# Eight router logits per token written with tokens on the partitions, two VectorE steps moved, and products that nobody reads in three waits of TensorE

## What is computed

```python
def moe_swiglu(h, router, w_in, w_out):
    logits = jnp.einsum('bnd,de->bne', h, router).astype(jnp.float32)
    top_logit, top_idx = lax.top_k(logits, TOP_K)          # TOP_K = 2 of N_EXPERTS = 8
    top_w = jax.nn.softmax(top_logit, axis=-1)
    gates = jnp.sum(jax.nn.one_hot(top_idx, N_EXPERTS, dtype=jnp.float32) * top_w[..., None], axis=-2)
    out = jnp.zeros_like(h)
    for e in range(N_EXPERTS):
        out = out + gates[..., e:e + 1].astype(h.dtype) * swiglu(h, w_in[e], w_out[e])
    return out
```

## Time and profile before

| | us |
|---|---|
| median of three runs | 1781.78 |
| lowest, highest | 1780.74, 1786.87 |
| the profiled execution, whole | 1783.62 |
| its span in the profile | 1781.9 |
| TensorE busy in it | 1682.8 (94%) |
| part from TensorE's last product before the norm to the end of the first expert's first four units | 820.4 to 863.8 |

### The profile page before, as it was taken

The page is one execution under the profiler, slowest core; times in us unless marked ns, Lnnn a source line. Parts: engine busy times, 40 slices in busy tenths (PEclk is TensorE's granted clock), DMA queues, the critical chain, the costliest instruction groups (busy, mean ns, idle before and its releaser), DMA issues.

```text
span 1781.9 us, 21700 instructions
## 1 busy us (share of the span) xinstructions
PE 1682.8 (94%) x8938; PEld 1166.2 (65%) x8939; DVE 782.7 (44%) x946; ACT 662.8 (37%) x716; POOL 277.1 (16%) x103
## 2 busy tenths in 40 slices
PE   5998798999999989997999999999999999999998
PEld 3576476778887869656665665656556665666664
DVE  3247524122223346455564545554554635434443
ACT  4222424122223245544353444443434524343432
POOL 0100012001001012001231212221222211111110
PEclk8999998999999999998999999999999999999999
DMA  9873721552222223122799999999999999899992
GB/s 373 311 293 148 273 98 48 189 189 95 95 95 95 65 100 117 50 71 96 265 410 409 409 398 409 409 408 407 400 409 408 409 403 375 313 348 350 362 366 97
DMA packets 158056, 470.66 MB, mean 264 GB/s; under 512 B 8473, under 2 KB 34178, under 8 KB 151298
## 3 DMA queue, kind: packets, MB, share of 16 engines
q1 hardware_dynamic: 154754, 463.28, 68.7%
q10 hardware_dynamic: 3200, 5.96, 1.0%
HBM read 468.13 MB, written 1.07 MB: 263 GB/s over the span
## 4 chain that ended last, share of the span: by engine, by line
PE 80%; ACT 5%; DVE 5%; POOL 4%; DMA 4%; issue 1%; SPq 0%; DVEq 0%; ACTq 0%
PE PS L329 15%; PE PS L331 14%; PE PS L330 14%; PE PS L2363 7%; PE PS L2378 4%; POOL low L310 4%; ACT high L301 3%; PE PS L2559 3%; PE PS L2298 3%; PE PS L2300 3%; PE PS L2299 3%; PE PS L1938 2%; PE PS L540 2%; PE PS L2548 2%; DVE low L310 1%
## 5 line engine op out<-in xcount | busy, mean ns | idle before, releaser
L310 DVE TENSOR_TENSOR low<-raw,high 128x2048 fp32r<-128x2048 f32 (+3 forms) x171 | 349.6, 2049 | 310.1 <-ACT high L301 309.8
L301 ACT ACTIVATE high<-raw 128x2048 fp32r<-128x2048 f32 (+2 forms) x171 | 323.6, 1894 | 410.6 <-PE PS L331 263.6
L329 PE MATMUL PS<-high,ah 128*128 128x512 f32 (+2 forms) x918 | 367.5, 400 | 16.2 <-DVE al L495 5.8
L330 PE MATMUL PS<-low,ah 128*128 128x512 f32 (+2 forms) x918 | 357.1, 389 | 0.0
L331 PE MATMUL PS<-high,al 128*128 128x512 f32 (+2 forms) x918 | 356.7, 389 | 0.0
L310 POOL TENSOR_TENSOR low<-raw,high 128x1024 fp32r<-128x1024 f32 (+2 forms) x56 | 182.0, 3249 | 1070.1 <-ACT high L301 1056.2
L329 PEld LDWEIGHTS PS<-high,ah 128*128 128x128 f32 x918 | 173.8, 189 | 91.5 <-issue 38.8
L331 PEld LDWEIGHTS PS<-high,al 128*128 128x128 f32 x918 | 173.9, 189 | 35.8
L330 PEld LDWEIGHTS PS<-low,ah 128*128 128x128 f32 x918 | 174.2, 190 | 31.5
L329 PE MATMUL PS<-ah,high 128*128 128x512 f32 x368 | 144.5, 393 | 1.8 <-DVE low L310 1.8
L331 PE MATMUL PS<-ah,low 128*128 128x512 f32 x368 | 143.3, 389 | 0.0
(11 more groups left out here) (388 smaller groups left out, 1882.4 us busy)
## 6 DMA issues: line engine op xcount, KB each, us to landing
raw<-in_moe_w_in_dram SPq DMA_DIRECT2D x150, 1024.0 KB, 13.5
raw<-in_moe_w_out_dram SPq DMA_DIRECT2D x75, 1024.0 KB, 12.2
raw<-in_ada_w_dram SPq DMA_DIRECT2D x48, 1024.0 KB, 8.3
X<-in_moe_w_in_dram SPq DMA_DIRECT2D x28, 1024.0 KB, 14.0
ah_behind<-in_moe_w_in_dram SPq DMA_DIRECT2D x25, 1024.0 KB, 13.2
raw<-in_ffn_w_in_dram SPq DMA_DIRECT2D x22, 1024.0 KB, 5.2
al_behind<-in_moe_w_in_dram SPq DMA_DIRECT2D x21, 1024.0 KB, 13.6
al_behind<-in_moe_w_out_dram SPq DMA_DIRECT2D x16, 1024.0 KB, 13.1
```

The lines of the kernel that those rows point to most:

```text
L301: act.activation(high[n % SPL][:, 0:width], buf[:, 0:width], ACT.Copy).then_inc(high_made, 1)
L310: eng.tensor_tensor(low[n % SPL][:, c0:c1], buf[:, c0:c1], high[n % SPL][:, c0:c1].bitcast(F32), ALU.subtract).then_inc(low_made[n % SPL], 1)
L329: pe.matmul(o, sh, mh, start=start, stop=False)
L330: pe.matmul(o, sh, ml, start=False, stop=False)
```

## The change

Four edits. (1) The logits are multiplied the other way round: the tokens' chunk (128 columns) is stationary, the router's 8 columns move, once for each block of tokens, so that the sum is written as 128 x 16 at once; the copy L1568 and the turn L2263 are gone. (2) `xn` is written before the chunks are scaled and not after the mask. (3) `rank_experts`, with the copy of the counts, is called after `gather_first` and not inside it. (4) `array_busy` multiplies the identity by 256 columns of `X` into a bank that nobody reads: 8 times when block 0 of X is ready, 2 times after the logits, once after the counts.

```diff
             norm_dve(dve, 2, lambda b: ps_rows(3 * b), lambda b: GGm, link)
+            for b in range(LB):
+                dve.tensor_scalar(xn[:, b, :], X[:, b, :], sc[:, RSTD + b:RSTD + b + 1], None, ALU.mult)
             pre_dve_chunks(dve, 3)
...
             dve.wait_ge(s["logits_done"], 1)
-            dve.tensor_copy(lT, PS[0:NE, 0, 0:SEQ]).then_inc(s["lt_copied"], 1)
-            dve.wait_ge(s["logits_turned"], 1)
             link(dve.tensor_copy(rs[:, LOG:LOG + 16], PS[:, 1, 0:16]))
...
-            for b in range(LB):
-                dve.tensor_scalar(xn[:, b, :], X[:, b, :], sc[:, RSTD + b:RSTD + b + 1], None, ALU.mult)
             dve.wait_ge(s["route_exp"], 1)
...
-            link(dve.tensor_copy(cnt, PS[:, 2, 16:24]))
             def rank_experts():
+                link(dve.tensor_copy(cnt, PS[:, 2, 16:24]))
...
-            gather_first(0, 0, 0, 0, rank_experts)
+            gather_first(0, 0, 0, 0)
+            rank_experts()
             dve.wait_ge(s["route_ready"], 1)
...
+            def array_busy(bank, n):
+                for _ in range(n):
+                    pe.matmul(PS[:, bank, 0:SEQ], ident, X[:, 0, 0:SEQ], start=True, stop=True)
+
+            x_ready(pe, 3, 0)
+            array_busy(2, 8)
             pre_pe(pe, 3)
             pe.wait_ge(s["rt_ready"], 1)
             for k in range(KD):
                 low_ready(pe, 3, k)
-                last = product(pe, PS[0:NE, 0, 0:SEQ], RTh[:, k, :], RTl[:, k, :], ahk[:, k, 0:SEQ], alk[:, k, 0:SEQ], k == 0, k == KD - 1)
+                for b in range(LB):
+                    last = added_product(PS[:, 1, NE * b:NE * (b + 1)], ahk[:, k, b * P:(b + 1) * P], alk[:, k, b * P:(b + 1) * P],
+                                         RTh[:, k, :], RTl[:, k, :], k == b == 0)
             last.then_inc(s["logits_done"], 1)
-            pe.wait_ge(s["lt_copied"], 1)
-            for b in range(LB):
-                last = pe.transpose(PS[:, 1, NE * b:NE * (b + 1)], lT[:, b * P:(b + 1) * P], K[0:NE, C_ID:C_ID + NE])
-            last.then_inc(s["logits_turned"], 1)
+            array_busy(2, 2)
...
             pe.matmul(PS[:, 2, 16:24], ones, mk[1], start=False, stop=True).then_inc(s["pos_done"], 1)
+            array_busy(3, 1)
```

More of the change, by code:

```diff
@@ L1856, in late_visit, with gather_first @@
                 gated("H", t, h)
-            def gather_first(v, h, e, pos, between=None):
+            def gather_first(v, h, e, pos):
                 select(e, pos).then_inc(s["sel_made"], 1)
-                if between:
-                    between()
                 low_units(v, h, 0, (0,))
```

## The result

| us | before | after |
|---|---|---|
| median of six runs | 1781.72 | 1796.07 |
| lowest, highest | 1778.00, 1786.87 | 1794.02, 1800.05 |
| the profiled execution, its span | 1783.62, 1781.9 | 1800.05, 1798.3 |
| from the start of L579 to the start of the light gather | 42.95 | 53.55 |

The ratio is 1.0061, with a 95% interval of 1.0042 to 1.0080: the changed kernel is 10.9 us slower, between 7.5 and 14.3. The prediction said 3.6 us slower, and at most 8.7.

What follows compares the result with a forecast made beforehand. TensorE, busy for 94% of the span, was taken as the bound. Unit 3 starting 2.0 us later plus 1.6 us lost to half clock gave +3.6 us, carried to the end: median 1785.4 us, range 1779.5 to 1790.5.

Steps and rivals of the forecast that it cites:

- The logits' start: Behind L540 and VectorE's chunks, the logits start 0.1 us earlier to 1.5 us later; 0.35 us later taken.
- The unread products: Ahead of L540, eight delay it 0.8 to 1.9 us but restore full clock; the later three cost nothing at full clock.
- The step that failed: At the gather, TensorE was taken at full clock: 3.77 us for 6.3 us.
- my upper bound 0.23: In the logits, each of the 48 narrow matmuls takes at most the half clock's 0.23 us; 0.114 was taken.
- half clock all through: Gather runs cold, or the first units do and GpSimd blocks the ranking's end: +6 to +9 us, chance 0.14.
- GpSimd's block: Near unit 3, GpSimd's half of unit 4 can hold VectorE up to 2.2 us; 0.2 taken.
- The first rival: In the logits, 8-column matmuls cost some 0.06 to 0.08 us, so less change than forecast: 1781.3 to 1783.8, chance 0.25.
- The late ranking: Units 1 and 2, ranking, load and selection precede unit 3: TensorE idles 4.9 us, unit 3 starts 2.0 us later.
- `xn`: Written early, within TensorE's first chunk from 827.1 to 828.5, it delays nothing there.
- SyncE's queue: Loads from the ninth on wait for the later ranking; idle DMA never caught up, 13 us later, 1795, chance 0.05.
- Carried to the end: From the light gather on, a shift before 882 us stays to the kernel's end, here 3.6 us.

Runs made afterwards that it cites:

- e4: The changed kernel with seven more unread 256-column products, one behind each of the logits' first seven chunks; ratio 1.0046 to the kernel before, L579 to light gather 50.90 us.
- e6: The kernel before with the narrow 8-column logits alone; ratio 1.0019, L579 to light gather 48.3 us.
- e5: The kernel before with only the ranking and the copy of the counts moved behind units 1 and 2; ratio 1.0035, L579 to light gather 49.7 us.
- e3: The changed kernel without the unread products; ratio 1.0054 to the kernel before, L579 to light gather 53.5 us.
- e1: The changed kernel with the old logits (24 matmuls of 256 columns, copy and turn); ratio 1.0031 to the kernel before, L579 to light gather 46.97 us.
- e11: The kernel before with early `xn`, the unread products and the ranking behind unit 3; ratio 1.0015, L579 to light gather 42.65 us.
- e13: The changed kernel with the ranking behind unit 3; ratio 1.0054 to the kernel before, L579 to light gather 50.9 us.
- e8: The kernel before with the unread products alone; ratio 0.9997, L579 to light gather 44.5 us.
- e12: The kernel before with early `xn` and the ranking behind unit 3, without unread products; ratio 1.0021, L579 to light gather 45.6 us.
- e2: The changed kernel with the ranking and the copy of the counts back at their old place; ratio 1.0020 to the kernel before, L579 to light gather 47.96 us.
- e7: The kernel before with the early `xn` alone; ratio 0.9986, L579 to light gather 42.46 us.
- e9: The kernel before with SyncE's ninth expert load also waiting for unit 2's lower half; ratio 0.9991, L579 to light gather 43.9 us.

## Why the prediction was wrong

**The logits' start held.** The unread products should end at 828.0 to 829.1 and the logits start 0.35 us late. In after, counted from L579 (3.03 us later there), L540 starts at 828.50 and the logits at 833.46, 0.18 us late.

**The step that failed** is one sentence: "TensorE has now worked for over 9 us with gaps under 1 us in the last three, so I take full clock." It took unbroken work to be enough for the gather, and the sum took full clock for all 48 narrow matmuls and the counts ahead of it. It isn't enough: 32 of the 48 narrow matmuls were through when the clock fell, with PE busy throughout. The price of one was right (0.111 us at full clock, 0.114 expected), and its double, 0.213, is what my upper bound 0.23 meant; I had given that to "half clock all through" with 0.14, whose 6 to 9 us come nearest by their causes, a cold gather and GpSimd's block, and are still too little. The first rival, 0.06 to 0.08 us for each (the prediction once calls it the second), is refuted by the 0.111. What the fall cost, by the terms of the sum:

| term | predicted | after | difference |
|---|---|---|---|
| logits' start behind L579 | 12.77 | 12.60 | -0.2 |
| 48 matmuls | 5.46 | 7.20 | +1.7 |
| T to the first expert, of it counts | 3.0 | 4.1 | +1.1 |
| and of it the gather | 3.77 | 6.16 | +2.4 |
| and of it the rest | 3.7 | 3.8 | +0.1 |
| units 1 and 2 on VectorE | 5.6 | 5.4 | -0.2 |
| ranking | 3.1 | 3.2 | +0.1 |
| `route_ready` to `select_light` | 1.0 | 1.1 | +0.1 |
| `select_light`, register loads | 1.5 | 1.7 | +0.2 |
| unit 3, with GpSimd's share | 2.5 | 3.9 | +1.4 |
| TensorE's unit 3 | 4.1 | 4.4 | +0.3 |
| sum | | | +7.0 |

With the predicted 3.6 that gives 10.6, which is what S grew by. Of the 7.0, 5.2 are the clock in the logits, the counts and the gather; the first expert, which was to start 1.8 us sooner, starts 3.3 us later (33.90 us behind L579 for 30.57). Experiments bear this out from both sides: e4 keeps the clock, and its S is 2.6 us shorter than after's although it has 3 us more to do; e6 has the narrow logits alone and 5.3 us more than before.

**GpSimd's block** was sized wrong within its own bound. I took 0.2 us and kept 2.2 for the range. VectorE's unit 3 started at 869.21, while GpSimd worked on unit 4 from 868.50 to 870.85, and took 3.81 us for 2.3. It held VectorE in every kernel with a late ranking, at whatever instruction it met: the selection in e5 and e3 (1.24 and 1.22 us for 0.35) and in e1 and e4 (2.20 and 2.22), a cast of the ranking in e11 to e13 (about 2 us for 0.17). So 0.9 to 2.2 us each time, and 0.2 in the sum. That unit 4's half falls due in these us had been written down; I should have counted most of it.

**The late ranking** was right in its mechanism: units 1 and 2, the ranking, the register load, the selection and unit 3 in a row, and TensorE idle before unit 3, 3.93 us in after and 4.65 in e5 (4.9 predicted). Its price was too small. Alone, e5, it costs 6.7 us of S, 6.0 of them behind the logits' start, and 0.35% of the time. There it doesn't have the 1.8 us on the first expert to set against, and the half clock behind the gap held for all of unit 3, 5.2 us.

**The unread products** cost nothing that can be told (e3, and the 0.9997 of e8), as said. That they would also give nothing was not said: in before the gather's half clock lies under VectorE's work on the ranking and unit 0, so its end at full clock would have been no use, and beside the narrow logits the clock is gone anyway. Only e11 against e12 has them at work, 2.7 us up to the first expert. Of the seven kernels with them the gather ran at full clock in e4 and e11, not in after, e2, e8 and e13 (6.03 to 6.16 us), and in part in e1 (4.88).

**`xn`**: predicted free; e7 gives 0.5 us less S, which is within the scatter. Right. **SyncE's queue**, the rival of 0.05, which would have given 1795 and so nearly the measured time: refuted by e9. A time that fits is no proof of its cause. **Carried to the end**: right, 10.5 us at 1025 and 10.2 at 1454.

**What stays open.** S scatters by about 1 us between kernels that ought to be alike (42.95 for before, 43.9 for e9). For most of that the place is known: in e3, e5, e6 and e9 the clock came back only near L540's end, and the logits start 13.2 us behind L579; in before, e7 and e12 it came back earlier, and they start at 12.3 to 12.4. Both groups have kernels with the early `xn` and without it, so none of the edits decides it. Counted from the logits' start on, e5 costs 6.0 us and e6 4.5, together 10.5, and after 10.4: the two costs add up. What is not placed is e8's 1.4 us behind the logits' start, which after doesn't show; why the clock comes back sooner in one profile than in another is open too.

## What to carry over

Ask of each stretch not only whether TensorE is busy but with what: before a wide matmul is turned into several narrow ones, take the stretch and what follows it at either clock, and put both into the sum. When a step is moved off one waiting place, list everything behind it in the new queue up to the next consumer, that is unit 3, then the selection, then the light gather here, with the other engine's half that falls due at the same time. And compare a short, fixed stretch beside the whole time, but let it end behind the last consumer: e11 looked like a gain since its stretch ended at the start of the gather that paid for it.

## What the runs showed of the chip

**The granted clock fell under continuous work.** In after it went from 0.99 to 0.50 at 840.1 in the 33rd of 48 matmuls of 8 columns, PE and PEld both busy all the time, and it fell in the logits of all five kernels with this stream unbroken. The Trainium skill (TensorE: Matmul & The Clock Gate, Part 1: The HAM clock gate (the "warmup" mystery)) has the clock set by how busy TensorE has been. The trace agrees for the gaps (unit 3 in e5, at 0.50 behind 4.65 us of idle time), and not in the sense in which the profile counts busy: its busy share was 1.00 ahead of this fall.

**A matmul of 8 columns with a load of 128 took a ninth of a microsecond.** With a stationary operand of 128 columns one took 0.111 us at full clock in fp32r, the same as a float32 pass of the counts (0.114), and 0.213 at half clock. The Trainium skill (TensorE: Matmul & The Clock Gate, LDWEIGHTS (loading the stationary operand)) gives columns / 1.2 in ns for a load, by which 128 columns are an estimated 107 ns. That agrees with the row at full clock and not with the one at half clock; the 81 ns for each matmul in a stream of loads and 128-column products, from the same page's section on the back-to-back issue gap, were not reached: by them the logits would have taken an estimated 3.9 us, and they took 7.2.

**GpSimd can hold a small instruction of VectorE.** In e11, e12 and e13 the cast of 128 x 8 numbers took 1.98, 1.99 and 2.33 us for 0.17, and each time it ended within 0.03 us of GpSimd's half unit (2.40 us from 856.52, 863.69 and 860.00). The two instructions between GpSimd's start and the cast in e11 ran undisturbed (0.09 and 0.16 us). In e1, e3, e4 and e5 it was the selection's 128 x 128 `tensor_scalar` instead, 2.20, 1.22, 2.22 and 1.24 us for 0.35, which ended within 0.1 us of GpSimd's half unit too. Why these and not those, no run tells.
